# The stationary tiles of a split fp32 product, each family at its own distance from the streamed ones

## The reference

```python
def first_block(x, mem, ...):
    mem_h = rms_norm(mem, mem_norm_g)
    x = x + hybrid_mixer(rms_norm(x, mix_norm_g), w_in, ..., w_mix_out)
    x = x + memory_cross_attention(rms_norm(x, xa_norm_g), mem_h, w_xq, w_xkv, w_xo)
    x = x + conv_glu_ffn(rms_norm(x, ffn_norm_g), w_gate, w_up, ..., w_down)
    return rms_norm(x, final_norm_g)

def second_block(x, c, w_ada, ...):
    shift_m, scale_m, gate_m, shift_f, scale_f, gate_f = split(silu(c) @ w_ada + b_ada, 6)
    h = modulate(rms_norm_2(x, pre_norm_mix), shift_m, scale_m)
    o = concatenate([nsa_mixer(...), moba_mixer(...)]) @ w_o        # both from h @ w_in
    x = x + gate_m * rms_norm_2(o, post_norm_mix)
    h = modulate(rms_norm_2(x, pre_norm_ffn), shift_f, scale_f)
    f = square(relu(h @ w_up)) @ w_down
    return x + gate_f * rms_norm_2(f, post_norm_ffn)
```

## Time and profile before

| | |
|---|---|
| time, median of 3 runs | 2787.32 us (2786.48 to 2788.82) |
| span of the profiled execution | 2785.1 us |
| the rest of the median beside that span | 2.2 us |
| mean granted clock of TensorE | 0.993 |
| PE busy | 2725.2 us, 98% |
| PEld busy | 2329.5 us, 84% |
| DVE, ACT busy | 1772.1 us (64%), 1324.0 us (48%) |
| memory read | 575.66 MB, 207 GB/s over the span |

### The profile page before, as it was taken

The page is one execution under the profiler, slowest core; times in us unless marked ns, Lnnn a source line. Parts: engine busy times, 40 slices in busy tenths (PEclk is TensorE's granted clock), DMA queues, the critical chain, the costliest instruction groups (busy, mean ns, idle before and its releaser), DMA issues.

```text
span 2785.1 us, 34787 instructions
## 1 busy us (share of the span) xinstructions
PE 2725.2 (98%) x13302; PEld 2329.5 (84%) x13302; DVE 1772.1 (64%) x2025; ACT 1324.0 (48%) x1679; POOL 169.5 (6%) x132
## 2 busy tenths in 40 slices
PE   8999999999999999999999999998989999999998
PEld 8999988888888888888888799887868888888887
DVE  4477488776578888765555564547775756645455
ACT  5555444454445454434455454446455344344443
POOL 0001620000000000000000002720000000000000
PEclk9999999999999999999999999999999999999999
DMA  8554068887477777775555556640755866755553
GB/s 284 164 170 131 1 242 275 290 278 261 164 259 273 273 279 272 274 257 182 194 182 200 181 188 204 200 151 1 259 180 197 280 204 238 261 189 177 191 185 132
DMA packets 293266, 579.60 MB, mean 208 GB/s; under 512 B 9168, under 2 KB 46192, under 8 KB 292112
## 3 DMA queue, kind: packets, MB, share of 16 engines
q1 hardware_dynamic: 291296, 566.08, 60.4%
q0 software_dynamic: 1120, 8.57, 0.8%
q10 hardware_dynamic: 720, 3.15, 0.3%
HBM read 575.66 MB, written 2.10 MB: 207 GB/s over the span
## 4 chain that ended last, share of the span: by engine, by line
PE 95%; DVE 3%; ACT 1%; issue 1%; DMA 0%; SPq 0%; POOL 0%; DVEq 0%; ACTq 0%
PE GP L1006 28%; PE GP L1008 28%; PE GP L1007 28%; PE TA L959 2%; PE TB L959 2%; PE TB L607 1%; PE TB L426 1%; PE GP L401 0%; PE TA L1375 0%; DVE wlo L1960 0%; PE GP L1216 0%; PE TA L1216 0%; PE GP L1203 0%; DMA x<-in_x 0%; DVE x L2402 0%
## 5 line engine op out<-in xcount | busy, mean ns | idle before, releaser
L1960 DVE TENSOR_TENSOR wlo<-raw,whi 128x1024 fp32r<-128x1024 f32 (+2 forms) x904 | 1088.2, 1217 | 812.2 <-ACT whi L1468 803.2
L1468 ACT CAST whi<-raw 128x1024 fp32r<-128x1024 f32 (+2 forms) x904 | 923.7, 1029 | 1170.8 <-PE GP L1008 1109.5
L1006 PE MATMUL GP<-whi,hhi 128*128 128x512 f32 (+2 forms) x1792 | 689.9, 385 | 1.9 <-issue 1.4
L1008 PE MATMUL GP<-whi,hlo 128*128 128x512 f32 (+2 forms) x1792 | 681.6, 380 | 0.0
L1007 PE MATMUL GP<-wlo,hhi 128*128 128x512 f32 (+2 forms) x1792 | 680.8, 380 | 0.0
L1006 PEld LDWEIGHTS GP<-whi,hhi 128*128 128x128 f32 x1792 | 338.1, 189 | 52.2 <-issue 3.3
L1008 PEld LDWEIGHTS GP<-whi,hlo 128*128 128x128 f32 x1792 | 337.8, 188 | 52.0
L1007 PEld LDWEIGHTS GP<-wlo,hhi 128*128 128x128 f32 x1792 | 338.3, 189 | 50.5 <-issue 1.0
L1006 PE MATMUL GP<-whi,bhi 128*128 128x512 f32 x704 | 277.0, 393 | 0.2 <-DVE blo L2021 0.2
L1948 DVE SCALAR_TENSOR_TENSOR ada_acc<-raw,csig,ada_acc 128x512 f32<-128x512 f32 x360 | 270.3, 751 | 10.2
L1008 PE MATMUL GP<-whi,blo 128*128 128x512 f32 x704 | 274.6, 390 | 0.0
(11 more groups left out here) (437 smaller groups left out, 2578.2 us busy)
## 6 DMA issues: line engine op xcount, KB each, us to landing
raw<-in_w_up SPq DMA_DIRECT2D x108, 1024.0 KB, 5.4
raw<-in_w_down SPq DMA_DIRECT2D x108, 1024.0 KB, 5.1
raw<-in_w_ada SPq DMA_DIRECT2D x96, 1024.0 KB, 5.2
raw<-in_w_gate SPq DMA_DIRECT2D x44, 1024.0 KB, 5.3
raw<-in_w_in SPq DMA_DIRECT2D x48, 856.0 KB, 4.7
raw<-in_w_xkv SPq DMA_DIRECT2D x32, 1024.0 KB, 5.7
raw<-in_w_in SPq DMA_DIRECT2D x24, 1024.0 KB, 5.0
raw<-in_w_in SPq DMA_DIRECT2D x24, 864.0 KB, 4.7
```

What stands on the lines that cost most here:

```text
L1006: pe.matmul(o, ahi[:, kt, t], whi[r][:, k, 0:q.width], start=first, stop=False)
L1008: m = pe.matmul(o, alo[:, kt, t], whi[r][:, k, 0:q.width], start=False, stop=last)
L1468: nc.scalar.copy(whi[(2 * g + s) % NRING][:, :, 0:q.width], raw[j % NSLOT][:, 2 * s:2 * s + 2, 0:q.width])\
L1960: TTo(wlo[r][:, :, 0:q.width], raw[j % NSLOT][:, 2 * s:2 * s + 2, 0:q.width], whi[r][:, :, 0:q.width].bitcast(F32), ALU.subtract).then_inc ...
```

## The change

Ahead of `hlo` and of `tab` an unused tile of 32 bytes is allocated. `level` gets a second argument, an offset to the remainder, and six of the tiles are allocated with offsets of 64 to 448 bytes. No instruction, no order and no wait is touched.

```diff
         hhi = fixed("hhi", [P, KT, T], F32R)
+        fixed("hlo_shift", [P, 8])
         hlo = fixed("hlo", [P, KT, T], F32R)
+        fixed("tab_shift", [P, 8])
         cst = fixed("cst", [P, CONST.shape[1]])
         tab = fixed("tab", [P, TAB_W])
...
-        def level(at):
-            return at + (ring0 - at) % 4096
+        def level(at, shift=0):
+            return at + (ring0 + shift - at) % 4096
...
-        mhi = ar("mhi", [P, KT, T], F32R); mlo = ar("mlo", [P, KT, T], F32R)
+        ar.at = level(ar.at, 64); mhi = ar("mhi", [P, KT, T], F32R); ar.at = level(ar.at, 96); mlo = ar("mlo", [P, KT, T], F32R)
...
-        ar = Arena(); ar.at = level(arena0)
-        bhi = ar("bhi", [P, KT, T], F32R); blo = ar("blo", [P, KT, T], F32R)
-        fhi = nc.alloc_sbuf_tensor_at("fhi", [P, 24, T], F32R, offset=hh0); flo = ar("flo", [P, 24, T], F32R)
+        ar = Arena(); ar.at = level(arena0, 128)
+        bhi = ar("bhi", [P, KT, T], F32R); ar.at = level(ar.at, 192); blo = ar("blo", [P, KT, T], F32R)
+        fhi = nc.alloc_sbuf_tensor_at("fhi", [P, 24, T], F32R, offset=hh0); ar.at = level(ar.at, 256); flo = ar("flo", [P, 24, T], F32R)
...
-        ar.at = level(ar.at)
-        f2hi = ar("f2hi", [P, 16, T], F32R); f2lo = ar("f2lo", [P, 16, T], F32R)
+        ar.at = level(ar.at, 320)
+        f2hi = ar("f2hi", [P, 16, T], F32R); ar.at = level(ar.at, 448); f2lo = ar("f2lo", [P, 16, T], F32R)
```

## The result

The changed kernel takes 2829.91 us (2825.79 to 2833.85, 4 runs) against 2787.02 us: ratio 1.0151, 95% interval 1.0138 to 1.0163. I had forecast no change, with 2779 to 2806 us as the range. The time lies 24 us above its end.

The account below looks back on a forecast made before the run. PE's stream of product matmuls was taken to bound the kernel. Moved loads and the rest of the edit added 0 us to the 2785.1 us span; with 2.2 us around it the forecast was 2787.3 us, range 2779 to 2806.

Parts of the forecast that it names:

- What bounds the kernel: PE's stream of 10,848 product matmuls, 2407 us of 2785.1 us; the change can act only through their spacing.
- moved loads, 6560: Stationary-operand loads whose distance to whi and wlo changes; each nanosecond per load was worth 6.6 us, 0.24% of the time.
- The first test: Runs of 26 product matmuls: steps stay 0.22 or 0.23 us across eight remainders of 4096, so addresses cost nothing.
- The second test: Narrow products: 196.0 ns at 428 and 432 columns, so stream width doesn't set the pace; slower loads would show at once.
- The third test: Plain fp32 matmuls: 112.5 ns at 32 past a multiple of 512 against 111.9 ns at 0, within rounding.
- both rivals: Faster: offsets remove a collision of stationary and streamed reads, up to 62.8 us gained, chance 0.11. Slower: offsets cause stalls, 0.16.
- The value taken: 0 ns for each of the 6560 moved stationary loads in the products, 0 us in all.
- The ends of plus and minus 10.5 ns: Limits per wide moved matmul, 226.8 ns less the fp32 stream's 216.3 ns: 62.8 us gained or lost.
- my nearer 4 ns: Loss per moved load, the step between weight-load durations of 188 and 192 ns: 26.2 us over 6560 loads.
- The slower rival: Equal phase is good, so each offset load stalls the stream once: 4 ns each, 26.2 us, 2813.5 us; chance 0.16.
- The excess of 10.5 ns over the fp32 stream: Wide products' 226.8 ns against 216.3 ns; the faster rival called it a collision that offsets remove: 2724.5 us, chance 0.11.
- The rest of the edit: Shift of cst, tab and what lies behind, and writes to moved tiles: 0 us, with 1 us either way.

Follow-up runs that it names:

- e2: Kernel before with moved tiles at differing multiples of 256 bytes (hlo 256, f2 256/768, flo 1024 and others): 2786.53 us, ratio 0.9999.
- e1: Kernel before with high and low tiles of each family at equal offsets modulo 256 (h 32, m 64, b 128, f2 192): 2832.53 us, ratio 1.0171.
- e6: Kernel before with other offsets (h 96/96, flo 352, m 160/160, b 224/224, f2 64/256) and qTx 64 bytes further from kTx: 2841.37 us, ratio 1.0191.
- e9: Kernel before with only the narrow products (428, 432 columns) starting 40 columns into their buffers, distance 96 modulo 256: 2787.20 us, ratio 0.9995.
- e3: Kernel before with only low tiles offset (hlo 64, mlo 96, blo 128, flo 192, f2lo 32), high tiles at 0: 2826.28 us, ratio 1.014.
- e8: Kernel before with the four streamed wlo buffers 64 bytes further on, stationary tiles keeping their distance to whi modulo 256: 2827.87 us, ratio 1.0138.
- e4: Kernel before with only 64 unused bytes ahead of cst, all family tiles at remainder 0: 2785.95 us, ratio 1.0.
- e7: Kernel before with every tile, raw and ring included, 64 bytes further on, so all distances stay: 2787.83 us, ratio 1.0003.
- e5: Changed kernel with hlo alone put back to remainder 0, its 32 bytes moved behind it: 2806.46 us, ratio 1.0073 against the kernel before.

## Why the prediction was wrong

**What bounds the kernel: right.** PE's stream, and the loss is all in its steps; ACT's wide casts now wait 1007.7 us for PE in place of 961.0. The count of moved loads, 6560, was right too, but they are not the unit of the price.

**The first test: this is the step that failed.** "26 matmuls in a row already meet eight different remainders of 4096, all the multiples of 512. If a remainder cost a few nanoseconds the steps would differ." The eight are one and the same remainder of 256. The test varied what doesn't matter (e2: 0.9999) and held fixed what does (e1: 1.0171). The 390 or 391 ns in all five families had the same flaw, since all five lay at remainder 0. I had written that nothing below 512 was in the trace for the split product, and then let eight equal values outweigh it.

**The second test failed too.** Narrow products, I said, are where a slower load would be seen at once, since the width doesn't set their pace. But the trace of before has them at one distance only, so nothing could be seen in it of a slower one. At 96 both go to 193.4 ns (e6, e9): that the pace doesn't follow the width is true at either distance, and says nothing about addresses. I took an equality that holds with the effect and without it for a sign of its absence. And a price of the load alone was not to be seen there at once: `hlo` at 32 made the step 1.8 ns longer at 432 columns and 1.5 ns shorter at 428.

**The third test was of another operation.** The profile shows a plain fp32 matmul as two records, each of which takes 216.3 ns for 256 columns, about two cycles for a column (so the "32 fp32 matmuls" of the prediction are 32 records, of 16 matmuls); they don't react to 64 bytes (e6, L402). They said nothing of the split product, as the text conceded; yet they were entered against both rivals.

**The value taken.** 0 ns per moved load; measured 42.6 us / 6560 = 6.5 ns. The ends of plus and minus 10.5 ns held, my nearer 4 ns was short by 2.5. The slower rival had the right sign, and a price of 26.2 us for what cost 42.6; its account ("each load stalls the stream once") is wrong in its unit: in `h` the 1216 moved loads of 512-wide products cost 17.6 ns each and in `f` the 352 moved loads of `flo` nothing, and what a load costs depends on those beside it (e3). The excess of 10.5 ns over the fp32 stream was not a collision that an offset removes: seven other distances were tried, and no family of wide products has a mean below 226.8 ns.

**The two rules of the Trainium skill.** Its page "SBUF — State Buffer", section "Who interferes with whom", gives TensorE independent read ports for the moving operand and for LDWEIGHTS, and says that PE never waits on anyone. That an address can't matter was my conclusion from it, and e1 (1.0171) and e8 (1.0138) contradict the conclusion; whether the ports are independent no run here shows. That the rule's agreement with the eight remainders stood as support was the same mistake again. The page "TensorE: Matmul & The Clock Gate" of the Trainium skill, section "Back-to-back issue gap", gives about 216 ns for 512 columns as the gap of a single matmul. The fp32 records with 256 columns have the same 216 ns, while no run here brought a 512-column split product under 226.8 ns on average.

**The rest of the edit:** 0 us, right (e4).

**Shown and not shown.** Shown: the spacing depends on the distances between stationary blocks and streamed rows, with a period of 256 bytes, from either side, in every family, and only in float32r matmuls of those tried; it is not the address itself (e7), nor the work of DVE and ACT. Not shown: the mechanism. The natural one is that the two reads meet in the same part of the memory and one waits; that the steps repeat in a fixed cycle (in `h` after the change 232, 239, 229 ns over and over) fits it, but no run took the overlap of the two reads away. Whether it is the row that is streamed during a load or the row that the block is then used for is open too, since all rows share one distance in every run but e8. And it is open why 0 is the best distance tried for 512 columns but not for 428 and 432, where 96 (e6, e9) and the mixed distances of e8 have 193.4 ns.

## What to carry to other kernels

When a load of the next stationary operand runs beside a float32r stream, keep both operands' start addresses equal modulo 256 bytes, rather than letting the allocator decide: with rows of 512 columns this was worth 1.4 to 1.9% of the kernel's time here wherever all or most families were off it, without any instruction. For other widths try it: with 428 and 432 columns another distance was 0.7 to 2.5 ns a matmul better, too little to see in the time. Before taking equal rows for evidence that something doesn't matter, ask which remainders, widths or types they all share; a test of a period has to include steps below the period. And look for the effect of a change in all members of the pattern it touches, here the three matmuls of a product, and by their starts rather than their durations: after the change the record that got no longer was the one whose load was moved.

## What the runs showed of the hardware

- Mean spacing of float32r matmuls with 512 columns by distance modulo 256, high and low alike: 0: 226.8 to 227.2 ns (before, e2, e4, e7); 32, 64: 233.3 (e1); 96: 234.2 (e6); 128: 232.7 (e1); 160: 233.4 (e6); 192: 229.0 (e1); 224: 233.2 (e6).
- With high and low unlike, 0/64: 231.0, 0/128: 231.3, 0/192: 231.1 (e3), 64/0: 232.7 (e6), 64/96: 231.3, 64/192: 231.8 (after). These are not the means of the values above, weighted by loads.
- With 428 and 432 columns: 195.1 and 195.9 ns at 0, 193.4 and 196.8 at 32, 193.4 and 193.4 at 96. At 428 columns kernels with the same distance modulo 256 (before, e2, e4, e5, e7) lie between 194.1 and 195.5 ns, so differences of about 1 ns say nothing there; at 432 the same five agree within 0.1.
- Loads of stationary blocks in the products stay near 188 ns in the records (before, after and e1 188, e3 187 to 191); the loss shows in the starts of the matmuls.
